# Two heads of a chunk inverse on the array's other two quarters, four output weight buffers, and state stores issued by another queue

## The reference, cut to what matters

```python
proj = jnp.einsum('bsd,de->bse', rms_norm(x, p['pre_g']), p['w_in'])
def step(St, inp):                                  # the RWKV-7 group, 4 heads of 64
    r_t, k_t, v_t, w_t, kk_t, a_t = inp
    sa = jnp.einsum('bhij,bhj->bhi', St, kk_t)
    St = (St * w_t[:, :, None, :] - sa[..., None] * (kk_t * a_t)[:, :, None, :]
          + v_t[..., None] * k_t[:, :, None, :])
    return St, jnp.einsum('bhij,bhj->bhi', St, r_t)
...
x = x + rms_norm(jnp.einsum('bse,ed->bsd', mixed, p['w_out']), p['post_g'])
```

## Time and profile before

| quantity | value |
|---|---|
| median of 3 runs | 4021.25 us (4016.33 to 4023.86) |
| the profiled execution, its own time | 4023.54 us |
| its span in the profile | 4021.4 us |
| mean granted clock of PE | 0.971 of full speed |
| PE busy | 3727.1 us, 93% |
| PE weight loads busy | 2727.1 us, 68% |
| DVE, ACT, POOL busy | 46%, 34%, 4% |

### The profile page before, as it was taken

How to read it: one execution, slowest core, us unless ns; L and a number is a source line. 1 busy time by engine, 2 the same in 40 slices (tenths; PEclk the granted TensorE clock), 3 DMA queues, 4 the chain that set the end, 5 groups by cost and what they waited for, 6 DMA issues and landing times.

```text
span 4021.4 us, 73957 instructions
## 1 busy us (share of the span) xinstructions
PE 3727.1 (93%) x30760; PEld 2727.1 (68%) x30760; DVE 1832.4 (46%) x4051; ACT 1369.7 (34%) x3579; POOL 145.3 (4%) x278
## 2 busy tenths in 40 slices
PE   4978999999999999999789699999999999999996
PEld 3756767686867767586457477777767687676863
DVE  2544535454544535455325445353635454354542
ACT  1232333334242432434223324233333434234241
POOL 0000000000000000000000000000000000000000
PEclk8988999999999999999889899999999999999998
DMA  6323242423324142231433142524232241523213
GB/s 231 104 90 114 87 158 88 131 90 116 114 81 153 55 150 90 77 122 40 143 127 97 58 145 63 173 66 160 87 130 90 99 133 43 170 76 107 88 38 111
DMA packets 319401, 431.78 MB, mean 107 GB/s; under 512 B 26670, under 2 KB 276460, under 8 KB 318908
## 3 DMA queue, kind: packets, MB, share of 16 engines
q1 hardware_dynamic: 291672, 374.85, 29.0%
q0 software_dynamic: 11648, 41.95, 3.2%
q10 hardware_dynamic: 15748, 10.24, 0.9%
HBM read 405.22 MB, written 32.26 MB: 109 GB/s over the span
## 4 chain that ended last, share of the span: by engine, by line
PE 79%; DVE 7%; DMA 5%; ACT 3%; DVEq 3%; issue 2%; ACTq 0%; POOL 0%; SPq 0%; POOLq 0%
PE bank L656 71%; PE bank L660 7%; DMA wout<-in_w_out 5%; DVEq L1284 3%; DVE T L1388 1%; DVE ml L1640 1%; ACT PT L2291 0%; ACT Sm L2251 0%; DVE xin L1710 0%; ACT mix L2148 0%; ACT PT L2103 0%; DVE pr L1396 0%; DVE T L1391 0%; DVE T L1400 0%; DVE T L1398 0%
## 5 line engine op out<-in xcount | busy, mean ns | idle before, releaser
L656 PE MATMUL bank<-hT,win 128*128 128x256 f32 (+3 forms) x6912 | 1636.9, 387 | 4.5 <-ACT hT L2002 4.5
L656 PEld LDWEIGHTS bank<-hT,win 128*128 128x128 f32 (+1 forms) x6912 | 1271.9, 189 | 234.8 <-issue 40.6
L656 PE MATMUL bank<-wout,mix 128*128 128x512 f32 x1024 | 459.5, 599 | 34.9 <-DMA wout<-in_w_out 32.5
L656 PEld LDWEIGHTS bank<-wout,mix 128*128 128x128 f32 x1024 | 187.9, 190 | 285.0 <-issue 200.9
L656 PE MATMUL bank<-kv,Q 96*128 96x512 f32 (+3 forms) x640 | 277.2, 531 | 10.9 <-ACT mix L2017 10.9
L1640 DVE TENSOR_REDUCE ml<-bank 128x1 f32<-128x512 f32 (+3 forms) x320 | 195.3, 610 | 129.3 <-PE bank L656 118.3
L660 PEld LDWEIGHTS bank<-cst,Sm 128*128 128x128 f32 x1344 | 153.2, 140 | 140.9 <-issue 64.7
L660 PE MATMUL bank<-cst,Sm 128*128 128x128 f32 x1344 | 215.4, 282 | 27.0 <-ACT Sm L2251 19.1
L2251 ACT ACTIVATE Sm<-bank,ml 128x512 f32<-128x512 f32 (+3 forms) x320 | 199.7, 625 | 80.7 <-DVE ml L1645 71.6
L1699 DVE TENSOR_TENSOR st<-st 128x1 f32<-128x1 f32 (+1 forms) x34 | 5.4, 158 | 476.2 <-ACT mix L2148 474.7
L2017 ACT ACTIVATE mix<-bank 128x256 f32<-128x256 f32 x128 | 49.0, 383 | 328.3 <-PE bank L656 328.3
(11 more groups left out here) (438 smaller groups left out, 5563.8 us busy)
## 6 DMA issues: line engine op xcount, KB each, us to landing
win<-in_w_in SPq DMA_DIRECT2D x176, 1024.0 KB, 5.4
wout<-in_w_out SPq DMA_DIRECT2D x132, 512.0 KB, 4.3
xin<-out_xres SPq DMA_DIRECT2D x32, 1024.0 KB, 7.5
out_xres<-xin SPq DMA_DIRECT2D x16, 1024.0 KB
win<-in_w_in SPq DMA_DIRECT2D x16, 896.0 KB, 4.9
win<-in_w_in SPq DMA_DIRECT2D x16, 640.0 KB, 4.6
win<-in_w_in SPq DMA_DIRECT2D x16, 512.0 KB, 5.5
bon<-in_cache_mem_k SPq DMA_DIRECT2D x16, 256.0 KB, 3.8
```

Of the source, the lines that this page charges most:

```text
L656: return pe.matmul(out, lhsT, rhs, start=start, stop=stop, skip_group_check=True)
```

## The change

In the inverse, heads 2 and 3 are held crossed in the transposed part: `XI[j][:, 1]` of chunk c lies on partitions `half(1-c)` and so does its Q. The first product of these heads reads `half(c)` and writes `half(1-c)`, quarters (0,1) and (1,0), into another bank; the X Q product reads `half(1-c)` and writes `half(c)`. The order of heads becomes 0, 2, 1, 3. The transposed product stays on quarters (0,0) and (1,1). ACT's copy and DVE's update are split accordingly, and `values_of_chunks` moves from level 0 to level 4, behind ACT's last copy. The slices of `w_out` go through four buffers, the two new ones over `PT` and `XX`, which are free from `s_mo` on. The six stores of the final states move from ACT to SP.

```diff
+        woutq = [wout[:, 0, :], wout[:, 1, :], flat4(PT), flat4(XX)]
-        s_wo = [sig(f"w_out_loaded{i}", 16 * 4) for i in range(2)]
+        s_wo = [sig(f"w_out_loaded{i}", 16 * 2) for i in range(4)]
...
-                def out_weights(it, i):
-                    sp.wait_ge(s_wou.h, s_wou.at(it, max(i - 1, 0)))
+                def out_weights(it, ip, i):
+                    if i < 2:
+                        sp.wait_ge(s_wou.h, s_wou.at(it, 0))
+                    elif i < 4:
+                        sp.wait_ge(s_mo.h, s_mo.at(ip, 1))
+                    else:
+                        sp.wait_ge(s_wou.h, s_wou.at(it, i - 3))
                     k = OUT_ORDER[i]
-                    sp.dma_start(wout[:, i % 2, :], ...).then_inc(s_wo[i % 2].h, 16)
+                    sp.dma_start(woutq[i % 4], ...).then_inc(s_wo[i % 4].h, 16)
...
-                    out_weights(B.ot, 4)
+                    out_weights(B.ot, B.ip, 4)
+                    out_weights(B.ot, B.ip, 5)
...
                 store_rows(B.ot - 1, S - T)
+                sp.wait_ge(s_fpr.h, s_fpr.at(l, 1))
+                sp.dma_start(a["shift_p"]...)      # and conv_p, and st_p of four heads
                 sp.wait_ge(s_wou.h, s_wou.at(B.ot, 0))
                 last_weights(0)
...
+                def crossed(q, c):
+                    return 1 - c if q >= 2 else c
...
-                    for q in range(NH):
+                    for q in (0, 2, 1, 3):
                         for c in range(2):
-                            last = mm(PP[2 * j][half(c), q * 64:(q + 1) * 64], Om[j][half(c), q, :], XI[j][half(c), 0, q, :])
+                            o = PP[2 * j + q // 2][half(crossed(q, c)), (q % 2) * 64:(q % 2 + 1) * 64]
+                            last = mm(o, Om[j][half(c), q, :], XI[j][half(c), 0, q, :])
...
+                    for pair in ((0, 2), (1, 3)):
+                        for q in pair:
+                            for c in range(2):
+                                x, t = half(crossed(q, c)), (q % 2) * 64
+                                o = PP[2 * j][half(c), T + t:T + t + 64] if q >= 2 else PP[4 + j][half(c), t:t + 64]
+                                last = mm(o, XI[j][x, 1, q, :], Qs[j][x, q, :])
                         if lev < 4:
+                            for q in pair:
+                                for c in range(2):
+                                    x = half(crossed(q, c))
+                                    last = mm(PP[4 + j][x, T + q * 64:T + (q + 1) * 64], Qs[j][x, q, :], XI[j][x, 1, q, :])
...
                     first_product(lev, 1)
-                    if lev == 0:
+                    rest(B, 3)
+                    if lev == 4:
                         values_of_chunks()
-                    rest(B, 3)
...
-                        if n == 1:
-                            pe.wait_ge(s_xxr.h, s_xxr.at(ip, 10))
...
+                        if n == 0:
+                            pe.wait_ge(s_xxr.h, s_xxr.at(ip, 10))
...
-                    v.tensor_tensor(XI[j][:, 1, :, :], An[j], mlev[:, 0:1, :].broadcast_to([P, NH, 64]), MULT)
+                    v.tensor_tensor(XI[j][:, 1, 0:2, :], An[j][:, 0:2, :], mlev[:, 0:1, :].broadcast_to([P, 2, 64]), MULT)
+                    for c in range(2):
+                        Q, X = slice(64 * c, 64 * c + 64), slice(64 - 64 * c, 128 - 64 * c)
+                        v.tensor_tensor(XI[j][X, 1, 2:4, :], An[j][Q, 2:4, :], mlev[Q, 0:1, :].broadcast_to([64, 2, 64]), MULT)
...
-                        v.tensor_tensor(XI[j][:, 0:k, :, :], XI[j][:, 0:k, :, :], d, SUB).then_inc(s_xxr.h, 1)
+                        if lev < 4:
+                            v.tensor_tensor(XI[j][:, 1, :, :], XI[j][:, 1, :, :], d[:, 4:8, :], SUB)
+                        v.tensor_tensor(XI[j][:, 0, 0:2, :], XI[j][:, 0, 0:2, :], d[:, 0:2, :], SUB)
+                        d = PP[2 * j][:, T:T + P].rearrange("p (h t) -> p h t", t=64)
+                        v.tensor_tensor(XI[j][:, 0, 2:4, :], XI[j][:, 0, 2:4, :], d, SUB).then_inc(s_xxr.h, 1)
...
-                            act.activation(Qs[j], PP[2 * j][:, 0:T].rearrange(...), ACT.Copy).then_inc(s_qrd.h, 1)
+                            act.activation(Qs[j][:, 0:2, :], PP[2 * j][:, 0:P].rearrange(...), ACT.Copy)
+                            act.activation(Qs[j][:, 2:4, :], PP[2 * j + 1][:, 0:P].rearrange(...), ACT.Copy).then_inc(s_qrd.h, 1)
...
-                act.wait_ge(s_fpr.h, s_fpr.at(l, 1))
-                act.dma_start(a["shift_p"]...)      # and conv_p, and st_p of four heads
```

More of the change, by code:

```diff
@@ L557, in block @@
                         if g == 4:
-                            out_weights(B.ot, 0)
-                            out_weights(B.ot, 1)
+                            out_weights(B.ot, B.ip, 0)
+                            out_weights(B.ot, B.ip, 1)
                         if g == 6 and B.turns:
@@ L595, in in_weights @@
                         sp.dma_start(win[:, g % 2, k0:k1, 0:w], src[:, k0:k1, :]).then_inc(s_wi[g % 2].h, 16)
-                def out_weights(it, i):
-                    sp.wait_ge(s_wou.h, s_wou.at(it, max(i - 1, 0)))
+                def out_weights(it, ip, i):
[5 more added lines that the diff above has]
+                        sp.wait_ge(s_wou.h, s_wou.at(it, i - 3))
                     k = OUT_ORDER[i]
-                    sp.dma_start(wout[:, i % 2, :], a["w_out"][sl, k * P:(k + 1) * P, :].rearrange("a p n -> (a p) n")).then_inc(s_wo[i % 2].h, 16)
+                    sp.dma_start(woutq[i % 4], a["w_out"][sl, k * P:(k + 1) * P, :].rearrange("a p n -> (a p) n")).then_inc(s_wo[i % 4].h, 16)
                 def prompt_block(B, m, e):
@@ L607, in prompt_block @@
                     for i in range(2, 4):
-                        out_weights(B.ot, i)
+                        out_weights(B.ot, B.ip, i)
                     if B.block + 1 < NB:
                         in_weights(B.ip + 1, 1)
-                    out_weights(B.ot, 4)
+                    out_weights(B.ot, B.ip, 4)
+                    out_weights(B.ot, B.ip, 5)
                     if B.turns:
@@ L618, in prompt_block @@
                     sp.dma_start(xin[:, :, :], src).then_inc(s_xl.h, 16)
-                    for i in range(5, KD):
-                        out_weights(B.ot, i)
+                    for i in range(6, KD):
+                        out_weights(B.ot, B.ip, i)
                     if B.block == 0:
@@ L639, in _ @@
                 store_rows(B.ot - 1, S - T)
+                sp.wait_ge(s_fpr.h, s_fpr.at(l, 1))
+                sp.dma_start(a["shift_p"][sl, :].rearrange("a (n p) -> (a n) p", p=P), fst[0:7, 0:P]).then_inc(s_state.h, 16)
+                sp.dma_start(a["conv_p"][sl].rearrange("a k c -> (a k) c"), fst[0:2, P:3 * P]).then_inc(s_state.h, 16)
+                for h in range(NH):
+                    c = 3 * P + h * HD
+                    sp.dma_start(a["st_p"][sl, h].rearrange("a i j -> (a i) j"), fst[0:HD, c:c + 64]).then_inc(s_state.h, 16)
                 sp.wait_ge(s_wou.h, s_wou.at(B.ot, 0))
@@ L879, in values_of_chunks @@
                     pe.wait_ge(s_ntr.h, s_ntr.at(ip, 4))
+                    pe.wait_ge(s_qrd.h, s_qrd.at(ip, 10))
                     for j in range(2):
@@ L892, in second_product @@
                         pe.wait_ge(s_anr.h, s_anr.at(ip, j + 1))
-                    for q in range(NH):
-                        for c in range(2):
-                            o = PP[4 + j][half(c), q * P:(q + 1) * P]
-                            last = mm(o[:, 0:64], XI[j][half(c), 1, q, :], Qs[j][half(c), q, :])
+                    for pair in ((0, 2), (1, 3)):
[4 more added lines that the diff above has]
+                                last = mm(o, XI[j][x, 1, q, :], Qs[j][x, q, :])
                         if lev < 4:
-                            for c in range(2):
-                                o = PP[4 + j][half(c), q * P:(q + 1) * P]
-                                last = mm(o[:, 64:P], Qs[j][half(c), q, :], XI[j][half(c), 1, q, :])
+                            for q in pair:
+                                for c in range(2):
+                                    x = half(crossed(q, c))
+                                    last = mm(PP[4 + j][x, T + q * 64:T + (q + 1) * 64], Qs[j][x, q, :], XI[j][x, 1, q, :])
                     last.then_inc(s_xx.h, 1)
@@ L1087, in project_out @@
                     if B.prompt:
-                        pe.wait_ge(s_wo[i0 % 2].h, s_wo[i0 % 2].at(B.ip, 16 * (i0 // 2 + 1)))
+                        pe.wait_ge(s_wo[i0 % 4].h, s_wo[i0 % 4].at(B.ip, 16 * (i0 // 4 + 1)))
                     elif i0 == 0:
                         pe.wait_ge(s_wos.h, s_wos.at(B.l, s_wos.n))
-                    wo = wout[:, i0 % 2, :] if B.prompt else woutd[i0]
+                    wo = woutq[i0 % 4] if B.prompt else woutd[i0]
                     if k == 2:
@@ L2184, in level @@
                                 act.wait_ge(s_xx.h, s_xx.at(ip, (lev - 1) * 2 + j + 1))
```

(9 more changed lines are left out.)

3 lines of the change are left out of this document (1 added, 2 removed).

## The result

| kernel | median | lowest to highest | runs | profiled execution: own time, span |
|---|---|---|---|---|
| before | 4022.56 us | 4016.33 to 4026.82 | 4 | 4023.54, 4021.4 us |
| changed | 3905.82 us | 3904.19 to 3909.04 | 4 | 3909.04, 3907.2 us |

The ratio is 0.9712, with a 95% interval of 0.9695 to 0.9729: 116.7 us less. The prediction of 3917 us (104 less) was 11 us too high and lies inside the range of 3895 to 3960. The mean granted clock hardly moved, 0.971 before and 0.972 after. The kernel before has one execution more here than in the table ahead of the prediction, which gave 4021.25 us.

What follows compares the result with a forecast made beforehand. PE, busy 93% of the span, was taken as the bound. Levels 59, output weights 33 and layer ends 12 sum to 104 us, from 4023.5 to 3919.5, or 3917 us after 2.3 for the median; range 3895 to 3960.

Steps and rivals of the forecast that it cites:

- PE sets the levels: Inverse levels: PE does not wait today, so shorter products shorten the stage; net 3.7 us a block, 59 us in 16.
- A round on four quarters costs 0.1175 us: Inverse products: a round of four costs what a pair costs now, saving 4.7 us a block (3.8 to 5.0).
- no overlap: Rival, inverse levels: crossed rounds cost two pairs and the levels give nothing, 3976 us; chance 0.06.
- drained array: Rival, inverse levels: changing between diagonal and crossed pairs drains the array, 0.5 us a round, 4142 us; chance 0.03.
- The waits uncovered, 1.0 us a block: Inverse levels: PE waits for ACT 0.4, 0.45 and 0.15 us in levels 0 to 2, none for DVE (0.5 to 2.2).
- The output weights: Output projection: earlier requests for slices of `w_out` end PE's waits, gain 33 us, low end 20.
- 33 us of 32.5 waited plus restarts: Output projection: the gain sized from the 32.5 us in PE's list of waits, plus restarts.
- The loads collide: Rival, output projection: gathers, `win`, residual rows and slices collide, some 23 of 33 us stay lost, 3940 us; chance 0.08.
- The layer's end: Layer's end: without ACT's stores first, the product by X moves 6.8 us ahead; 6 us a layer, 12 us (6 to 14).
- The loss that I set aside for the clock: Layer's end: some of the 6.8 us is lost if the clock stays low for longer; 6 us a layer taken.
- The sum: Whole kernel: 59 + 33 + 12 = 104 us less, giving 3917 us; forecast given 0.68.

Runs made afterwards that it cites:

- e4_uncrossed: The changed kernel with the crossing taken out, all heads on quarters (0,0) and (1,1), the rest of the change kept: 3965.70 us, ratio 0.9857.
- e7b_dve_order: The changed kernel with DVE updating the inverse before its transpose, with a separate semaphore for the second products: 3902.85 us, ratio 0.9713.
- e8b_act_order: The changed kernel with ACT's copies of level 0 put before its copies of the first queries: 3900.19 us, ratio 0.9704.
- e2_wout: The kernel before with the four output weight buffers alone: 3976.83 us, ratio 0.9886.
- e6b_three_buffers: The changed kernel with three output weight buffers instead of four: 3904.57 us, ratio 0.9717.
- e3_stores: The kernel before with the state stores moved from ACT to SP alone: 4010.32 us, ratio 0.9971.
- e5b_order: The changed kernel with heads in the order 0, 1, 2, 3 and pairs (0, 1), (2, 3): 3907.80 us, ratio 0.9724.
- e9_both: The changed kernel with both reorderings, DVE's inverse before its transpose and ACT's level 0 copies before the first queries: 3896.42 us, ratio 0.9689.

## Why the prediction was right, step by step

**PE sets the levels.** Right. Shorter products came out as shorter levels, and the chunk steps behind them gave nothing back: in 16 blocks they took 338.4 us before and 338.7 after.

**A round on four quarters costs 0.1175 us.** Right. The first products went from 1.08 to 0.62 us, 0.46 less for four rounds, which is 8 x 0.1175 - 4 x 0.1175 = 0.47; the second products went from 2.01 to 1.55, the same 0.46. The rounds of the products in the earlier trace rows were a good price for a kind of round that the trace did not have. The rivals "no overlap" and "drained array" are excluded by these distances, and `e4_uncrossed`, 3965.70 us without the crossing, shows that the gain comes from it. By the rule of the Trainium skill (TensorE: Matmul & The Clock Gate, Part 3, The mechanism), weights load beside running matmuls only where the row group differs, and a crossed pair shares both row groups with the diagonal one; what the prediction drew from it, a round as long as two pairs, did not come: 16 matmuls take 0.62 us on four quarters against 1.08 on two.

**The waits uncovered, 1.0 us a block.** Right in sum, 0.3 + 0.36 + 0.27 = 0.93 us in the block quoted, but partly by luck: right in place for two of three, with one term too large and another put at nothing, which cancelled. Levels 0 and 1 wait for ACT, by 0.30 and 0.36 us where 0.4 and 0.45 were expected. The error is the pair of copies, taken as two full durations, 0.56 us; they overlap and end 0.44 us after the first starts (630.24 to 630.68). The Trainium skill (ScalarE: Activation LUTs, What ACT_TABLE_LOAD costs) says that successive ACTIVATEs overlap by about 93 ns; here they start 0.15 to 0.17 us apart at 0.28 each, so the trace agrees in kind, with an overlap of 0.11 to 0.13. In level 2 the prediction had 0.15 for ACT and nothing for DVE. It was the reverse: ACT in time, DVE late by 0.27 us, because the filler there is 0.6 us and not the 1.2 to 1.5 that I assumed from other levels. `e7b_dve_order` and `e8b_act_order` show both waits by removing them. Net of the levels: 57.9 us against 59.

**The output weights: the term that was mis-sized.** Predicted 33 us, measured 48.3 in the trace and 45.1 by itself in `e2_wout`. The mechanism was right, every slice is now in time. What failed is the step "33 us of 32.5 waited plus restarts": I took the list of waits for the whole loss. Idle time is counted from the end of the last matmul, and that end is modelled past the point where the next could have started: 16 matmuls have a duration of 7.05 us but the next starts after 6.89. So each stop costs about 0.17 us more than the listing says, and a slice that is late by less than that is not listed at all. The first matmul after a stop also takes 0.53 us to the next start instead of 0.43, another 0.10. In the block above that makes 3 x 0.27 = 0.81 us for three stops: 3.25 lost against 2.44 listed. In all 16 blocks 48.3 us stood against 32.5, and it was there to be read in the earlier trace rows: 526.88 - 518.80 = 8.08 us for two slices whose work takes 6.89, a loss of 1.19 with 1.02 shown. The prediction's 3.53 us for a slice comes from the same durations; from start to start it is 3.43. The prediction should have measured from start to start, as it did in the levels.

**The loads collide.** They didn't. `win` stands between slices 3 and 4 in SP's queue and costs nothing; `e6b_three_buffers` shows that even a buffer less leaves enough.

**The layer's end.** Right: 6.8 us earlier at `X,cst`, as worked out, 12 us predicted for the two layers, 11.0 measured in the trace and 11.6 in `e3_stores`. The loss that I set aside for the clock (6.8 to 6) was too small: 2.06 us go at once. At the end of the stage 1.0 us is missing in the first layer of the changed kernel, but 1.8 in `e3_stores`; what gave the rest back with the other edits in place, no run separates. The Trainium skill (DMA: Bandwidth & Descriptors, Issuing engines are not separate DMA queues) says that issuing from several engines saves only the sequencer's time, usually small beside the transfer. Here it was neither small nor all: six issues took ACT 4.0 us, and the product moved by 6.8, because ACT's wait for the final states stood ahead of its copies as well.

**The sum.** 59 + 33 + 12 = 104 was forecast; 57.9 + 48.3 + 11.0 less 3.0 elsewhere is 114.2 in the traces and 116.7 in the medians. Most of the 2.5 us between the two is the choice of the profiled executions: that of the changed kernel lies 3.2 us above its median, that of the kernel before 1.0 above its own.

## What to carry to other kernels

Where PE is the bound, measure a stall from start to start against the same group undisturbed; a list of waits misses the part that hides behind modelled ends, here a third of the loss. Small products that use two quarters of the array can be laid on all four if half of the operands are held on the other partitions; a round of four then takes the 0.12 us that a pair took. After that look at once at the engines that hand over between the products, since their order of work was hidden before. Do not let an engine that has to hand something to PE issue a store just before it.

## What the runs showed of the hardware that was not expected

- The order in which matmuls for different quarters are issued matters little: 0.67 us for the first products with both diagonal heads first, 0.62 interleaved, 1.08 without crossing. In `e5b_order` PE starts MATMULs for a free quarter ahead of six earlier ones for a busy quarter.
- Issuing a store from ACT's queue takes 0.49 us as a rule, and now and then much longer: 1.83 us once in the kernel before, up to 2.06 in `e9_both`, for the same 32 KB store of rotary keys. Why is open.
- Two buffers of 512 KB, each 3.4 us of use, were not enough with a landing of 4.3 us, three, with 6.9 us from request to use, were with a landing of 5.3, and a fourth gave nothing.
- Work that started sooner met the low clock: the stretch at 1.2 GHz became shorter (13.6 us for 17.2) but ended 5.9 us after the product by X instead of 1.5, and 2.06 us of the 6.83 gained went there at once.
